# Sparse attention inside a long transformer kernel: probabilities scaled before they are turned, one PSUM accumulator a pair of heads, another order of copies, weights and small transpositions

## What is computed

```
s_c = q @ k_cmp.T - slope * distance        # 31 compressed blocks of keys
p_c = softmax(masked s_c);  o_c = p_c @ v_cmp
s_s, p_s, o_s   # the same over selected key blocks; 16 may be selected and there are 8, so all are
s_w, p_w, o_w   # the same over a window of 512, so again all causal keys
o = g0 * o_c + g1 * o_s + g2 * o_w          # gates g, a sigmoid per token, head and branch
out = o @ w_out
softmax: p = exp(s - max);  p / max(sum(p), 1e-30)
```

## Time and profile before

| | us |
|---|---|
| median of three runs | 3489.71 |
| the profiled execution | 3483.9 |
| its span, first to last instruction | 3482.2 |
| TensorE busy in the span | 3398.7 (98%) |
| VectorE busy | 2411.0 (69%) |
| ScalarE busy | 1472.3 (42%) |
| attention's steps: first scores to the last V2 | 646.6 to 861.5 |

### The profile page before, as it was taken

The page is one execution under the profiler, slowest core; times in us unless marked ns, Lnnn a source line. Parts: engine busy times, 40 slices in busy tenths (PEclk is TensorE's granted clock), DMA queues, the critical chain, the costliest instruction groups (busy, mean ns, idle before and its releaser), DMA issues. The chain is left out here.

```text
span 3482.2 us, 56148 instructions
## 1 busy us (share of the span) xinstructions
PE 3398.7 (98%) x21983; PEld 2867.9 (82%) x21983; DVE 2411.0 (69%) x3238; ACT 1472.3 (42%) x2096; POOL 1065.8 (31%) x687
## 2 busy tenths in 40 slices
PE   8999999999999999999999999999999999999998
PEld 6889988645889978997777789988998888878997
DVE  6687774466777777786567587778777534468786
ACT  5644442465444453333544343344333422244333
POOL 1243322010243235443024045524542100015452
PEclk9999999999999999999999999999999999999999
DMA  3333334100223223333200133322322222213331
GB/s 122 97 101 106 103 105 97 37 1 13 97 98 106 99 85 98 108 101 98 64 26 8 57 103 104 108 85 97 110 96 97 85 85 85 85 58 103 107 101 69
DMA packets 232580, 296.26 MB, mean 85 GB/s; under 512 B 21893, under 2 KB 201464, under 8 KB 232392
## 3 DMA queue, kind: packets, MB, share of 16 engines
q1 hardware_dynamic: 230864, 290.48, 25.6%
q0 software_dynamic: 1152, 3.05, 0.4%
q10 hardware_dynamic: 376, 0.12, 0.0%
HBM read 291.53 MB, written 2.10 MB: 84 GB/s over the span
## 5 line engine op out<-in xcount | busy, mean ns | idle before, releaser
L337 DVE TENSOR_TENSOR wlo<-raw,whi 128x2048 fp32r<-128x2048 f32 x266 | 660.3, 2482 | 278.2 <-ACT whi L331 249.2
L331 ACT ACTIVATE whi<-raw 128x2048 fp32r<-128x2048 f32 x178 | 340.8, 1915 | 639.7 <-PE bank L343 549.2
L341 PE MATMUL bank<-u_hi,whi 128*128 128x512 f32 x1440 | 563.3, 391 | 4.2 <-DVE arena L3498 2.4
L343 PE MATMUL bank<-u_hi,wlo 128*128 128x512 f32 x1440 | 561.5, 390 | 0.0
L342 PE MATMUL bank<-u_lo,whi 128*128 128x512 f32 x1440 | 560.9, 389 | 0.0
L341 PE MATMUL bank<-h_hi,whi 128*128 128x512 f32 (+1 forms) x1340 | 536.0, 400 | 22.2 <-DVE h_lo L1136 9.9
L343 PE MATMUL bank<-h_hi,wlo 128*128 128x512 f32 (+1 forms) x1340 | 522.1, 390 | 0.0
L342 PE MATMUL bank<-h_lo,whi 128*128 128x512 f32 (+1 forms) x1340 | 522.1, 390 | 0.0
L509 PE MATMUL bank<-th,whi 128*128 128x256 f32 x1408 | 394.5, 280 | 2.3 <-DVE tmp L745 2.3
L511 PE MATMUL bank<-th,wlo 128*128 128x256 f32 x1408 | 392.8, 279 | 0.0
L510 PE MATMUL bank<-th,whi 128*128 128x256 f32 x1408 | 392.8, 279 | 0.0
(11 more groups left out here) (494 smaller groups left out, 6377.3 us busy)
## 6 DMA issues: line engine op xcount, KB each, us to landing
raw<-in_ffn_wgu SPq DMA_DIRECT2D x88, 1024.0 KB, 5.1
raw<-in_ffn_wd SPq DMA_DIRECT2D x44, 1024.0 KB, 4.8
raw<-in_mlp_w_up SPq DMA_DIRECT2D x32, 1024.0 KB, 5.3
raw<-in_mlp_w_down SPq DMA_DIRECT2D x32, 1024.0 KB, 4.8
raw<-in_odd_w_in SPq DMA_DIRECT2D x24, 1024.0 KB, 5.1
raw<-in_even_w_in SPq DMA_DIRECT2D x13, 1024.0 KB, 5.3
raw<-in_rg_w_in SPq DMA_DIRECT2D x8, 1024.0 KB, 5.3
raw<-in_odd_w_out SPq DMA_DIRECT2D x8, 1024.0 KB, 5.0
```

Source lines behind the costliest of these rows:

```text
L331: e.activation(whi[:, n % 2, :], raw[:, n % 2, :], ACT.Copy).then_inc(hi_ready, 1)
L337: e.tensor_tensor(wlo[:, n % 2, :], raw[:, n % 2, :], whi[:, n % 2, :].bitcast(F32), ALU.subtract).then_inc(lo_ready, 1)
L341: pe.matmul(o, w_hi, r_hi, start=first, stop=False)
L343: return pe.matmul(o, w_lo, r_hi, start=False, stop=last)
```

## The change

1. `weigh` runs once for each query block (**W0..W3**): reciprocal of two sums, then min with 1e30 times the gates, into `wq`. The probabilities themselves are then multiplied in place before they are turned: **A0..A3** (`scale_a`, ScalarE, head 0) and **B0..B3** (`scale_b`, VectorE, head 1). T0 now waits for all A and B of its step.
2. Since the dense branches and the compressed one are then all weighted, bank 5 or 6 (by pair) accumulates all three. `spread`, `take_spread`, `combine`, `pick`, `osum`, `oadd` go. High and low read the bank.
3. Ts loses its two extra columns and runs once a pair, into the other pair's output bank, so it waits for the **low** part of the pair before (`o_lo`). Vc accumulates in the output bank.
4. K2 of head 1 goes from ScalarE to VectorE. On ScalarE, K comes ahead of X of the same i.
5. Scores rotate over four banks (7, 0, 1, 2) from step 1 on, in place of three.
6. For the compressed branch, the subtraction of the maximum and the two products into `mt` go from VectorE to GpSimd; the reduction and the clamp (**SH**, `shift_cmp`) stay on VectorE, behind W3 and B3.

In TensorE's queue a step is then S0, S1, [Ts in even steps], V2, T0, S2, T1, V0, [Vc in even steps], S3, T2, V1, [C in even steps]. VectorE: M0, M1, K0, W0, B0, M2, K1, W1, B1, [WC in odd steps], W2, M3, B2, K2, [MC in even steps], W3, B3, [SH in even, low in odd steps]. ScalarE: X0, K0, X1, A0, [take_small in even; exp of the compressed scores and high in odd steps], K1, X2, A1, A2, X3, K2, A3.

The core of the diff:

```diff
@@ pool_nsa
-            chain(e.memset(pick, 1.0))
...
+            for j in range(PAIRS):
+                e.wait_ge(cx_dve, j + 1)
+                e.tensor_tensor(flat, flat, cmx.unsqueeze(2).broadcast_to([P, 8, NC]), ALU.subtract).then_inc(cx_pool, 1)
+                e.wait_ge(cq_dve, j + 1)
+                if j:
+                    e.wait_ge(mt_pe, j)
+                for hd in range(2):
+                    ins = e.tensor_tensor(mt[:, :, 32 * hd:32 * hd + NC], cs[:, hd, :, 0:NC],
+                                          csum[:, 4 * hd:4 * hd + 4].unsqueeze(2).broadcast_to([P, QT, NC]), ALU.mult)
+                ins.then_inc(mt_pool, 1)
+                if j + 2 < PAIRS:
+                    biases(j + 2)
@@ turn
                             if g == 0:
-                                pe.wait_ge(ex_act, 8 * n + 2 * q + hd + 1)
+                                pe.wait_ge((na_scaled, nb_scaled)[hd], 4 * n + q + 1)
@@ values
-                        ins = pe.matmul(pbank[5 + n % 2][hd * HD:hd * HD + HD, k * P:S], v[:, k, G * HD:G * HD + HD],
-                                        probT[hd][:, K_AT[k]:K_AT[k] + (QT - k) * P], start=k == 0, stop=k == QT - 1)
+                        ins = pe.matmul(pbank[5 + j % 2][hd * HD:hd * HD + HD, k * P:S], v[:, k, G * HD:G * HD + HD],
+                                        probT[hd][:, K_AT[k]:K_AT[k] + (QT - k) * P], start=n % 2 == 0 and k == 0,
+                                        stop=n % 2 == 1 and k == QT - 1)
@@ turn_small, spread
-            def turn_small(n):
-                pe.wait_ge(mt_dve, n + 1)
-                if n:
-                    pe.wait_ge(rs_act, n)
+            def turn_small(j):
+                pe.wait_ge(mt_pool, j + 1)
+                if j:
+                    pe.wait_ge(o_lo, j)
...
-            def spread(n):
-                pe.wait_ge(ms_act, n + 1)
-                pe.matmul(pbank[7][:, :], pick, ms[VR:VR + 2, :], start=True, stop=True).then_inc(rr_pe, 1)
@@ the loop of pe_nsa
-                    if i == 0 and n >= 2:
-                        spread(n - 2)
+                    if i == 1 and n % 2 == 0:
+                        turn_small(n // 2 - 1)
+                    if n >= 2 and i == (1 if n <= STEPS else 0):
                         values(n - 2, 2)
@@ act_nsa
+            def scale_a(n, q):
+                part = prob[n % 2][0][:, Q_AT[q]:Q_AT[q] + (q + 1) * P]
+                e.wait_ge(wq_dve, 4 * n + q + 1)
+                e.activation(part, part, ACT.Copy, scale=wq[:, n % 2, 2 * q:2 * q + 1]).then_inc(na_scaled, 1)
@@ dve_nsa
+            def weigh(n, q):
+                w = wq[:, n % 2, 2 * q:2 * q + 2]
+                e.wait_ge(ex_act, 8 * n + 2 * q + 2)
+                chain(e.reciprocal(w, sums[:, n % 2, 2 * q:2 * q + 2]))
+                e.scalar_tensor_tensor(w, w, 1e30, gates_of(n, 1 + n % 2)[:, q, :], ALU.min, ALU.mult).then_inc(wq_dve, 1)
+
+            def scale_b(n, q):
+                part = prob[n % 2][1][:, Q_AT[q]:Q_AT[q] + (q + 1) * P]
+                e.wait_ge(wq_dve, 4 * n + q + 1)
+                e.tensor_scalar(part, part, wq[:, n % 2, 2 * q + 1:2 * q + 2], None, ALU.mult).then_inc(nb_scaled, 1)
...
-            def combine(n):
-                e.wait_ge(rs_act, n + 1)
-                e.wait_ge(pv_pe, 3 * n + 3)
...
+                    if i == 3 and n >= 3 and n % 2:
+                        j = (n - 3) // 2
+                        e.wait_ge(o_hi, j + 1)
+                        e.tensor_tensor(rg_low(j), pbank[5 + j % 2][:, :], rg_high(j).bitcast(F32), ALU.subtract)\
+                            .then_inc(o_lo, 1)
```

More of the change, by code:

```diff
@@ L1726, in build @@
         unit_no = {}
-        for n_ in range(STEPS + 1):
-            keys = [(n_, q_, hd_) for q_ in range(QT) for hd_ in range(2)] if n_ < STEPS else []
+        for n_ in range(STEPS):
+            keys = [(n_, q_, hd_) for q_ in range(QT) for hd_ in range(2)]
             if n_ % 2 == 0:
-                keys[4:4] = [(n_, "o")] if n_ else []
-                keys += [(n_, "c", 0), (n_, "c", 1)] if n_ < STEPS else []
+                keys += [(n_, "c", 0), (n_, "c", 1)]
             for key in keys:
                 unit_no[key] = len(unit_no)
+        unit_bank, bank_before, last_in = [], [], {}
+        for key, v_ in unit_no.items():
+            b_ = v_ % 3 if key[0] == 0 else (7, 0, 1, 2)[(v_ - 10) % 4]
+            unit_bank.append(b_)
+            bank_before.append(last_in.get(b_))
+            last_in[b_] = v_
         def head_of(n, hd):
@@ L1779, in pool_nsa, with biases @@
             chain(e.memset(gz[:, :, NC:NC + 1], 0.0))
-            chain(e.memset(pick, 1.0))
[L1781 to L1785, removed]
+            def biases(j):
                 if j == 1:
@@ L1843, in free_bank @@
             def free_bank(v):
+                for u in (v - 1, v):
+                    if bank_before[u] is not None:
+                        last = bank_before[u]
                 if v >= 3:
-                    pe.wait_ge(sc_dve, v - 2)
+                    pe.wait_ge(sc_dve, last + 1)
             def scores(n, q):
@@ L1928, in values @@
                 pe.wait_ge(pa_act, 3 * n + g + 1)
[L1929 to L1934, removed]
+                pe.wait_ge(pb_dve, 3 * n + g + 1)
+                if g == 0 and n % 2 == 0 and j:
+                    pe.wait_ge(ms_act, j)
                 for k in GROUPS[g]:
@@ L1988, in pe_nsa @@
                             values(n - 1, i - 2)
-                        if i == 2:
-                            turn_small(n - 1)
+                        if i == 2 and n % 2 == 0:
+                            values_cmp(n // 2 - 1)
                     if i == 3 and (n, "c", 0) in unit_no:
@@ L2089, in act_nsa @@
[L2089 to L2096, removed]
-                    if i == 2 and n >= 3 and n % 2:
+                    if i == 3 and n <= STEPS:
+                        take_turned(n - 1, 2)
+                        if n == STEPS:
+                            act_hi(e, n0 + 11)
@@ new lines, in act_nsa @@
+                    if i and n < STEPS:
+                        if i < 3:
+                            scale_a(n, i - 1)
+                        if i >= 2:
+                            scale_a(n, i)
+                    if i == 1 and n % 2 == 0:
+                        take_small(n // 2 - 1)
+                    if i == 1 and n % 2 and n < STEPS:
+                        e.wait_ge(cx_pool, n // 2 + 1)
+                        e.activation(cs[:, :, :, 0:NC], cs[:, :, :, 0:NC], ACT.Exp).then_inc(cx_act, 1)
@@ L2148, in masked_cmp @@
             def masked_cmp(n):
[L2149 removed]
+                if n:
+                    e.wait_ge(mt_pool, n // 2)
                 for hd in range(2):
@@ L2213, in dve_nsa @@
                     if i in (1, 2) and 1 <= n <= STEPS:
-                        if i == 1:
-                            if n % 2:
-                                weigh_cmp(n - 1)
-                            weigh(n - 1)
                         take_turned(n - 1, i - 1)
-                    if i == 1 and n >= 2:
-                        combine(n - 2)
-                    if i == 3:
-                        if n >= 3 and n % 2:
-                            j = (n - 3) // 2
-                            e.wait_ge(o_hi, j + 1)
-                            e.tensor_tensor(rg_low(j), osum, rg_high(j).bitcast(F32), ALU.subtract).then_inc(o_lo, 1)
-                        if (n, "c", 0) in unit_no:
-                            masked_cmp(n)
+                    if i in (1, 2) and n < STEPS:
+                        weigh(n, i - 1)
+                        scale_b(n, i - 1)
+                    if i == 2 and n < STEPS:
+                        if n % 2:
+                            weigh_cmp(n - 1)
+                        weigh(n, 2)
+                    if i == 3:
+                        if n < STEPS:
+                            scale_b(n, 2)
+                        if 1 <= n <= STEPS:
+                            take_turned(n - 1, 2)
+                        if n < STEPS:
+                            if (n, "c", 0) in unit_no:
+                                masked_cmp(n)
+                            weigh(n, 3)
+                            scale_b(n, 3)
+                            if (n, "c", 0) in unit_no:
+                                shift_cmp(n)
+                    if i == 3 and n >= 3 and n % 2:
[3 more added lines that the diff above has]
+                            .then_inc(o_lo, 1)
             dve_out(e, "nsa_out", True, stage)
```

115 lines of the change are left out of this document (41 added, 74 removed).

## The result

| kernel | median us | runs | lowest to highest |
|---|---|---|---|
| before | 3489.53 | 6 | 3487.99 to 3493.3 |
| changed | 3464.62 | 6 | 3463.47 to 3467.14 |

The ratio of changed to before is 0.9928, with a 95% interval of 0.9915 to 0.9941. 24.9 us went, where 22.5 were forecast (3467.2). In the first set of experiments, the changed kernel took 3462.44 and the kernel before 3489.11.

A forecast was written before the change was run, and what follows sets the result against it. TensorE was nearest bound; afterwards a dependency ring of 22.0 us a pair. 22.8 us to step 16's T0 plus 0.5 behind, less 0.8 for the clock: 22.5, median 3489.7 to 3467.2; own range 3462 to 3473, wider 3457 to 3480.

The forecast's parts named there:

- TensorE's 2.66 us: TensorE's queue, each pair: two `spread` and one Ts go, 2.66 us less, leaving 19.4 busy or 19.0 without overlaps.
- VectorE's and ScalarE's work: Engine work per attention pair after the change: VectorE 18.5 us, almost TensorE's; ScalarE about 15.8, no bound.
- the sign of 18 to 19: Sign that the prediction is right: VectorE busy for 18 to 19 us a pair.
- the row that was taken: Profile row used for B: in-place SBUF multiply by a per-partition scalar, 480 ns for 512 columns.
- the row of 616 ns: Profile row used for A on ScalarE: 616 ns for 512 columns, less 0.1; 2.9 us a pair for eight A.
- The ring, step by step: Chain of dependencies across engines from one even step's T0 to the next: 22.0 us, against 24.3 to 25.6 before.
- The 0.35 us for GpSimd: Added to 21.65 us because B3 of the odd step falls among GpSimd's bias operations and both hold each other up.
- The rival with 14 us of gain: B3 waits up to 1.5 us within GpSimd's second bias operation: period 23.2, gain 14 us, 3476; chance 0.18.
- The clock: Rival: TensorE's 1.9 us stand brings the lower clock, pairs about 34 us, gain eaten from two on; chance 0.05.
- The first T0: T0 of step 1, after step 0's W3, B3 or A3 end by 662.0: at 662.1, against 663.42 before.
- the last T0: T0 of step 16 after seven periods of 22.0: 825.7 against 848.50, 22.8 us gained; behind it another 0.5 less.
- 0.8 us aside for the clock: Taken back from 23.3 us of gain in case stretches at the lower clock, seen in the profile before, come again.

The follow-up runs named there:

- the kernels at 19.26 us: Two kernels: low right behind M3 and C ahead of T2 on the changed kernel, with GpSimd's bias after B3 (3441.06 us) or left where it was (3442.73 us).
- the run without scaling: Changed kernel with W, A and B not issued and T0 waiting for the exps alone; does not compute the result: 3439.35 us, 0.9858 of before.

## Why the prediction was right, point by point

**TensorE's 2.66 us.** Right in kind, and somewhat small: 22.03 busy in a pair at full clock before, 18.88 after, 3.2 less (19.4 worked out). 19.04 us is the pair when nothing else holds it, against 19.0 worked out.

**VectorE's and ScalarE's work.** VectorE has 17.7 us a pair, 0.8 under the 18.5 worked out and just under the sign of 18 to 19. W's two operations stand 0.20 us apart (740.05 to 740.25), so W is about 0.40, not 0.44; B runs at the pace of the row that was taken. ScalarE has 17.1 us, 1.3 over the 15.8 worked out: A takes 722 ns for 512 columns and 394 for 128, where the row of 616 ns, less an overlap, was taken for it. That term was too small, but ScalarE sets nothing in this ring. B by shape, where `tmp` is head 1's tile in odd steps:

```profile
L2192 DVE TENSOR_SCALAR fsum<-fsum,arena 128x512 f32<-128x512 f32 x8 | 3.9, 486 | 0.3
...
L2192 DVE TENSOR_SCALAR tmp<-tmp,arena 128x128 f32<-128x128 f32 x8 | 2.3, 287 | 0.3
```

**The ring, step by step.** T0 of the odd step comes 10.35 us behind the even one (670.35 to 680.70; 10.4 worked out), and the even one 21.54 us behind, at full clock (21.65 worked out). TensorE stands 1.94 us ahead of Ts (1.9). MC waits 0.56 for C (0.5). A move of Ts or of low shortened the ring to 20.12 and 19.86 (20.1 each, worked out before they ran). This is shown, not argued.

**The 0.35 us for GpSimd.** The term was too large. B3 of the odd step beside a bias takes 590 ns against 486:

```profile
755.73 3.21 POOL L1790 TENSOR_SCALAR arena<-arena 128x512 f32<-128x512 f32 x2 [0.97 <-DVE arena L2151]
...
757.01 0.59 DVE L2192 TENSOR_SCALAR tmp<-tmp,arena 128x512 f32<-128x512 f32 x1
```

That 0.10 us is on the changed kernel's ring. GpSimd has no bias left to compute in the last two pairs, B3 takes 0.49 there (803.25, 824.70), and the periods that end with them are 23.03 and 21.45 us, against 23.11 and 21.54 where a bias is beside B3. Only in the kernels at 19.26 us, where TensorE is nearly the bound, is it off the ring. The row behind the term was misread as well: 1.93 us is from one bias operation's start to the next, and undisturbed ones start 1.55 apart (in the run without scaling), so the bias had grown by 0.38 us, not 0.44.

With low ahead of it, B3 starts later and takes 0.83 us. Here, from the run with low behind M3, are both bias operations (they begin at 706.77 and 708.32) beside B2 and B3:

```profile
706.77 3.04 POOL L1790 TENSOR_SCALAR arena<-arena 128x512 f32<-128x512 f32 x2 [0.98 <-DVE arena L2151]
...
707.21 0.41 DVE L2192 TENSOR_SCALAR tmp<-tmp,arena 128x384 f32<-128x384 f32 x1
...
708.38 0.83 DVE L2192 TENSOR_SCALAR tmp<-tmp,arena 128x512 f32<-128x512 f32 x1
```

By the rule of the Trainium skill, page "SBUF — State Buffer", section "Who interferes with whom", the later of two such operations waits for the whole of the other. The trace does not bear that out: B2 begins 0.44 us into the first bias and takes its usual 0.41, and B3 begins 0.06 us into the second and ends 0.6 us before it does. The two engines hold each other up by 0.1 to 0.35 us, not by a whole operation; what sets the amount is open. (The profile's spans of GpSimd are rough; two undisturbed bias operations take 3.04 us in each pair of the run without scaling.) The rival with 14 us of gain, which needed a wait up to 1.5 us here, did not come.

**The clock.** This is the mechanism that was mis-sized. It stood among the rivals as one that makes the change slower, with 0.05, for whole pairs at the lower clock. What came is a stretch of 3 to 4 us behind the new wait, in three to four pairs of six, 1.6 us each, and one more behind the 3.37 us wait of step 16. These the wait brings: with the wait filled, or taken away by a move of Ts or of low, the granted clock is 1.00 from step 4 on. The forecast's reading of before was short, though. It counts two low stretches there, and there are four: the one of T0 in step 1 and the three shown above, which come with no wait of over 0.8 us in their pairs. So a long wait is one way to a low stretch and not the only one. The profiled execution of the changed kernel has 6 of them, its other one 4, the kernel before 4: not all that the low clock costs the changed kernel is a cost that it added. (The forecast's sum for a clock that is low throughout does not add up either: seven pairs of 34 us in place of 22 are 84 us, 3551 and not 3560.)

**How the parts made the sum.** The first T0 came as forecast (662.1 less the 2.0 us by which this execution's attention started sooner; 659.88), the second 0.6 late, with a T0 at the lower clock (1.84 us). Of the last T0, forecast for 825.7 and seen at 827.26 plus 2.0: 6.3 us from four low stretches and 0.6 from the first, less 3.2 from the 0.46 us by which the period was over-estimated (0.25 of it GpSimd's term). Behind the last T0, 18.1 us were forecast and 19.4 came, 18.56 before: T0 of step 16 ran at the lower clock (827.26, halves of 1.09 and 1.06 us). The forecast had set 0.8 us aside for the clock in all. The attention gave 18.4 us in this pair of profiles, not 22.5. The median gave 24.9 because the profiled execution of before was 5.6 us under its own median, and that of after 1.0 over it. So that the forecast is near the median is partly luck: the ring was taken too long and the clock too cheap, and the profile of before was a fast one. The mechanism is borne out by the periods rather than by the total. Within a set, runs of the kernel before differ by up to 7 us and their granted clock by 0.003 to 0.004, the slower ones having the lower clock; low stretches are the likely cause, but where they lie in those runs was not looked at.

**What the gain is made of.** I gave it to TensorE's lighter queue, with the fourth bank as a side remark. At full clock a pair went from 24.34 to 21.54 us: 3.2 us less work on TensorE and 0.4 us more waiting. But the lighter queue pays only with the fourth bank: without it the change loses 0.26%. And the forecast's list of waits left out the largest, those of `turn` for K; between 676 and 848 us of the kernel before they are

```profile
PE bank L1922 <- DVE tmp L2193: 4.4, 6, 0.8
PE bank L1922 <- ACT tmp L2062: 3.3, 11, 0.3
```

and none of them is left in the changed kernel. No run has the fourth bank alone or the new order of K and X alone on top of the kernel before, so how the gain divides among queue, bank and order is not shown.

## What to carry to other kernels

Work out the ring of waits with each engine's order written out, and ask of every new wait what stands behind it in that queue: Ts needed the low part, V2 and T0 did not, and they stood 1.9 us behind it. Putting an operation that nobody needs soon behind the urgent ones, or its producer ahead of work that can wait, gave some two thirds of what the whole change gave (14.6 and 16.4 against 24.9 us). Count a buffer (here a fourth PSUM bank) as part of an edit's price or worth of its own, since the same instructions with three banks were a loss.

## What the runs showed of the hardware that was not expected

- TensorE's wait of 1.94 us costs more than its length: in three to four of six pairs V2 and T0 behind it ran at the lower of the two clocks (granted 0.55 over 3.8 us; T0 at 715.26 in 1.97 us, at 738.13 in 1.09). Twelve idle transposes in that gap took 1.53 us of it and saved 5 us of the run.
- Low stretches also come without such a wait: three in seven pairs of the kernel before, each behind 4.6 us of which TensorE was busy for 4.1 to 4.2.
- A VectorE operation that begins within a GpSimd operation is not held until that is over: B of 512 columns took 0.59 and 0.83 us in place of 0.49 beside a bias of 1.49 to 1.59 us, and B of 384 columns its usual 0.41.
- With three banks and waits of up to 2.9 us the granted clock over five pairs is 0.88.
- W's second operation, on two columns, takes 0.38 us in place of 0.16 where it meets GpSimd's two products (754.04).
